# 32 more tokens leave the dense U products, and ScalarE multiplies the gates into the one-hots

## The chip, the cores and the metric

The kernel runs on one core of one Trainium2 chip. The metric is the device time of one execution in microseconds (us); lower is better. Engines are named as in the profile: PE is TensorE (PEld its weight loads), DVE is VectorE, ACT is ScalarE, POOL is GpSimd, SP is the engine that issues most transfers.

## The reference, cut to what matters

512 tokens of width 1024 pass two layers. Each layer is an attention block (three groups of heads) and then a PEER channel mixer. The change touches only the mixer:

```python
q = (xc @ w_q).reshape(c, 8, 2, 128)
sc = einsum('chpd,hpnd->chpn', q, sub_keys)
top_s, top_i = top_k(sc, 16)
cand = top_s[:, :, 0, :, None] + top_s[:, :, 1, None, :]
cand_s, cand_i = top_k(cand.reshape(c, 8, 256), 16)
experts = i1 * 128 + i2                 # 128 of 16384 experts for a token
gates = softmax(cand_s)
ue, ve = u[experts], v[experts]         # rows of 1024 floats
act = gelu(einsum('chkd,cd->chk', ue, xc))
return einsum('chk,chkd->cd', gates * act, ve)
```

Each token uses 128 of the 16384 rows of U and V (8 heads, 16 a head; a "slot" is one of them).

## The kernel before, in words

Tokens lie in four blocks of 128 partitions. Block 0 is computed sparsely: for each of its 128 slots one indirect transfer fetches 128 rows of U (one a token, 512 KB), and VectorE forms the 128 dot products with the tokens in one instruction (`row_dot`, L1508 and L1565). The other 384 tokens (`TN`) are computed densely: all 16384 experts in 128 blocks of 128 (`experts`, L2031). One block is 24 matmuls of 128x128 by 384 columns: eight chunks of the model width, times three products of high and low halves (`stationary`, L2005, L2006, L2009). A block needs its weights from HBM (SP, 512 KB), a cast of them by ScalarE (L979), their remainder by GpSimd (L705), and afterwards a Gelu by ScalarE (`gelu`, L1022), whose result SP stores to `gelu_d` (192 KB).

The order of work in one layer, written out by hand on each engine's queue:

1. The query products and scores; VectorE begins the selection (`unit`, L1423, 32 units: one of a head and a token block). Units 0 to 7 are of block 0, and their row numbers are made at L1494.
2. The PRE stage: 44 pairs of expert blocks on TensorE. VectorE does the other 24 units with four dots of gathered U rows in each (96 slots); GpSimd issues those gathers between its remainders, eight rows in flight (`zone`).
3. The gates: softmax of the chosen scores, `gate_ready` at L1537; TensorE turns the row numbers and the gates of the 384 tokens into columns (L2045), with the last block of the pair (`experts(PRE, 1)`) behind them; ScalarE keeps them in `i_t` and `g_t`.
4. Twelve bodies of 32 tokens (eight groups of four). They write a dense gate matrix: VectorE makes for each token two one-hot rows (`one_hots`, L1549: `oh_2` by L1556, and `oh_1` by L1559, which multiplies the gate in), TensorE multiplies them (`spread`, L2050), ScalarE copies the result to `g_stage` (`keep_gates`, L1061 and L1102). Spreads use two PSUM banks in turn, and the one-hots a ring of four groups. Bodies 0 to 7 (`B_ROUNDS`) also hold four expert blocks each, one after every second group, and four dots of gathered U rows (slots 96 to 127, `gather_b`, `b_row`, four rows in flight). Bodies 8 to 10, here called late, hold two expert blocks each, and ScalarE sets one PSUM bank after each (L1097). Body 11 holds no expert block. In bodies 2 to 9, the staged gates of the window before (two bodies are a window) go to HBM in two transfers of 1 MB a body on ScalarE's queue (L1072).
5. The V stage: 128 blocks of 18 matmuls by 512 columns (L2096), with the gates times the Gelus as stationary operand (`gated`, L1591, reads `h_in` and the gates); block 0's V rows are gathered and added by VectorE (L1615). Then a layer norm.

## Time and profile before

| | |
|---|---|
| Median of 3 runs | 3270.34 us (3270.07 to 3271.58) |
| The profiled execution's own time | 3272.12 us |
| Its span in the profile | 3270.3 us |
| Granted TensorE clock, mean | 0.992 |
| Busy share: PE, PEld, DVE, ACT, POOL | 97%, 88%, 78%, 40%, 60% |
| Moved by transfers | 765.22 MB, mean 234 GB/s |

The busy share of TensorE is modelled from pipelined instructions: each matmul's time overlaps the next one's, so the rate has to be read from start to start. The two layers repeat one pattern; layer 0's mixer fills about 360 to 1625 us of the span, layer 1's about 1990 to 3250 us. PEclk is the granted clock as a share of full speed; the DMA share is the mean busy share of 16 DMA engines.

### The profile page before, as it was taken

What the parts mean: (1) busy time and instruction counts of PE and PEld (TensorE: products, weight loads), DVE (VectorE), ACT (ScalarE), POOL (GpSimd) and SP (SyncE); (2) the same over time, 40 slices, a digit from 0 to 9 for tenths busy, and PEclk for the clock granted to TensorE, in tenths of its full rate; (3) what the DMA queues carried; (4) which work ended last, traced back from release to release, by engine and by line L of the source; (5) the groups of instructions that cost most, each with busy time, mean ns of one, the idle gap of its engine ahead of it and who ended that gap; (6) DMA issues with size and microseconds to landing.
All of it is one profiled execution on the core that took longest, in us unless ns stands there. A gap on an engine that the chain in (4) does not pass through costs nothing. (4 is left out here: it accounts for less than half of the span.)

```text
span 3270.3 us, 64230 instructions
## 1 busy us (share of the span) xinstructions
PE 3173.4 (97%) x18582; PEld 2886.0 (88%) x18582; DVE 2537.1 (78%) x5431; ACT 1306.9 (40%) x2080; POOL 1958.6 (60%) x1556
## 2 busy tenths in 40 slices
PE   8998999999999999999999999999999999999997
PEld 8878889999999888888798787999999998888886
DVE  1475658888888899999925746588888888999998
ACT  2464234444444333333324643344444443333332
POOL 3454348888654466666545543488885535666665
PEclk9999999999999999999999999999999999999999
DMA  4002139999787699999820021499997867999996
GB/s 162 36 2 78 54 107 321 319 320 319 244 297 252 245 338 337 339 335 335 281 103 26 2 78 61 131 320 319 321 319 243 290 241 276 338 338 337 337 333 225
DMA packets 249405, 765.22 MB, mean 234 GB/s; under 512 B 28384, under 2 KB 95712, under 8 KB 241376
## 3 DMA queue, kind: packets, MB, share of 16 engines
q1 hardware_dynamic: 170400, 459.95, 42.6%
q0 software_dynamic: 73728, 268.47, 22.0%
q10 hardware_dynamic: 5184, 35.65, 3.1%
q8 instruction: 47, 0.77, 0.1%
q14 instruction: 46, 0.38, 0.0%
HBM read 677.98 MB, written 85.98 MB: 234 GB/s over the span
## 5 line engine op out<-in xcount | busy, mean ns | idle before, releaser
L705 POOL TENSOR_TENSOR st_lo<-st_raw,st_hi 128x1024 fp32r<-128x1024 f32 x290 | 698.1, 2407 | 463.2 <-ACT st_hi L979 457.4
L979 ACT CAST st_hi<-st_raw 128x1024 fp32r<-128x1024 f32 x544 | 569.9, 1048 | 662.9 <-PE ps L2096 638.0
L2005 PE MATMUL ps<-t_hi,st_hi 128*128 128x384 f32 (+1 forms) x2288 | 794.4, 347 | 0.0
L2006 PE MATMUL ps<-t_lo,st_hi 128*128 128x384 f32 (+1 forms) x2288 | 786.2, 344 | 0.0
L813 POOL TENSOR_TENSOR wt_lo<-w_f,wt_hi 128x384 fp32r<-128x384 f32 x256 | 417.9, 1633 | 319.5 <-ACT wt_hi L1110 319.4
L2009 PE MATMUL ps<-t_hi,st_lo 128*128 128x384 f32 (+1 forms) x2288 | 462.6, 344 | 0.0
L2005 PEld LDWEIGHTS ps<-t_hi,st_hi 128*128 128x128 f32 x2288 | 430.0, 188 | 10.2
L2006 PEld LDWEIGHTS ps<-t_lo,st_hi 128*128 128x128 f32 x2288 | 430.1, 188 | 10.0
L2009 PEld LDWEIGHTS ps<-t_hi,st_lo 128*128 128x128 f32 x2288 | 408.5, 188 | 10.9
L1022 ACT ACTIVATE h_out<-ps 128x384 f32<-128x384 f32 x256 | 125.9, 492 | 695.4 <-PE ps L2009 614.5
L2096 PE MATMUL ps<-st_hi,wt_hi 128*128 128x512 f32 x1536 | 390.6, 390 | 2.7 <-ACT wt_hi L1110 2.7
L2096 PE MATMUL ps<-st_lo,wt_hi 128*128 128x512 f32 x1536 | 390.7, 390 | 0.0
L2096 PE MATMUL ps<-st_hi,wt_lo 128*128 128x512 f32 x1536 | 389.7, 389 | 0.0
L1606 DVE TENSOR_TENSOR st_lo<-st_raw,st_hi 128x1024 fp32r<-128x1024 f32 x252 | 308.8, 1225 | 74.5 <-ACT st_hi L979 74.5
L2096 PEld LDWEIGHTS ps<-st_hi,wt_hi 128*128 128x128 f32 x1536 | 288.5, 188 | 63.5 <-issue 3.7
L2096 PEld LDWEIGHTS ps<-st_lo,wt_hi 128*128 128x128 f32 x1536 | 289.2, 188 | 60.2
L2096 PEld LDWEIGHTS ps<-st_hi,wt_lo 128*128 128x128 f32 x1536 | 288.3, 188 | 59.8
L1615 DVE SCALAR_TENSOR_TENSOR ps<-v_row,w_sp,ps 128x1024 f32<-128x1024 f32 x256 | 326.9, 1277 | 0.5
L1596 DVE TENSOR_TENSOR w_f<-g_ch,h_in 128x256 f32<-128x256 f32 x250 | 303.2, 1213 | 5.2 <-DMA h_in<-gelu_d 3.4
L724 POOL DMA_INDIRECT v_row<-in_peer_v,idx_v x256 | 248.7, 972 | 43.2 <-issue 9.2
L1559 DVE TENSOR_SCALAR oh<-ps,i_t,g_t 128x128 f32<-128x128 f32 x768 | 261.1, 403 | 0.0
L1508 DVE CUSTOM_DVE_ANT_0 u_row<-ps,u_row 128x1024 f32<-128x1024 f32 x192 | 232.3, 1210 | 35.8 <-DMA u_row<-in_peer_ur,idx_u 35.6
(222 smaller groups left out, 4969.1 us busy)
## 6 DMA issues: line engine op xcount, KB each, us to landing
st_raw<-in_peer_u SPq DMA_DIRECT2D x256, 512.0 KB
st_raw<-in_peer_v SPq DMA_DIRECT2D x256, 512.0 KB
gelu_d<-h_out SPq DMA_DIRECT2D x256, 192.0 KB
h_in<-gelu_d SPq DMA_DIRECT2D x256, 192.0 KB
gates_d<-g_stage ACTq DMA_DIRECT2D x32, 1024.0 KB
g_ch<-gates_d SPq DMA_DIRECT2D x56, 512.0 KB, 6.1
w_raw<-in_w_in SPq DMA_DIRECT2D x16, 1168.0 KB, 5.3
st_raw<-in_peer_w_q SPq DMA_DIRECT2D x32, 512.0 KB
```

What stands on the lines that cost most here:

```text
L705: nc.gpsimd.tensor_tensor(st_lo[:, s].rearrange("p c f -> p (c f)"), st_raw[:, r], st_hi[:, s].rearrange("p c f -> p (c f)").bitcast(F32), ...
L724: nc.gpsimd.indirect_dma_start(out=dst, out_offset=None, in_=table, in_offset=bass.IndirectOffsetOnAxis(ap=number, axis=0)).then_inc(lande ...
L813: nc.gpsimd.tensor_tensor(wt_lo[:, s], w_f[:, s], wt_hi[:, s].bitcast(F32), ALU.subtract).then_inc(wt_l, 1)
L979: nc.scalar.copy(st_hi[:, r % 2].rearrange("p c f -> p (c f)"), st_raw[:, r]).then_inc(st_h, 1)
L1559: last = nc.vector.tensor_scalar(oh_1[:, GRP * r + k], iota_ps, i_t[:, 0, ds(t0 + k, 1)], g_t[:, ds(t0 + k, 1)], ALU.is_equal, ALU.mult)
L1596: nc.vector.tensor_tensor(w_f[:, s, 0:T_D].rearrange("p (w o t) -> p w o t", w=2 * WIN_D, o=1), gates, h_in[:, s, 0:T_D].rearrange("p (w o ...
L1606: nc.vector.tensor_tensor(st_lo[:, s].rearrange("p c f -> p (c f)"), st_raw[:, r], st_hi[:, s].rearrange("p c f -> p (c f)").bitcast(F32), ...
L1615: nc.vector.scalar_tensor_tensor(out=acc, in0=v_row[:, r], scalar=w_sp[:, ds(b, 1)], in1=acc, op0=ALU.mult, op1=ALU.add).then_inc(v_acc, 1)
L2005: nc.tensor.matmul(dst, st_hi[:, s, c], t_hi[:, c, rows], start=c == 0, stop=False)
L2006: nc.tensor.matmul(dst, st_hi[:, s, c], t_lo[:, c, rows], start=False, stop=False)
L2009: last = nc.tensor.matmul(dst, st_lo[:, s, c], t_hi[:, c, rows], start=False, stop=c == DC - 1)
L2096: last = nc.tensor.matmul(ps[:, 2 * d + 2 + half], w[:, s, d * P:(d + 1) * P], v[:, half * 512:(half + 1) * 512], start=False, stop=True, ...
```

## The change

The last 32 tokens of block 3 (`XT`) leave the dense U products, which then have 352 columns (`TU`). Their 128 slots are laid out four side by side: partition 32g+t holds slots 32g to 32g+31 of token t, so that 32 more gathers of 128 rows fetch all of them. Dot products go from 128 to 160; the 64 that fall into bodies 0 to 7 are now eight a body. The numbers and the tokens for this layout are moved by eight small transfers from ScalarE's queue before the first body, the results back by four after body 8. Gate times Gelu of those tokens is then put where their gates stood (`g_t`), and their columns of the stored Gelus are ones; the V stage is as before.

The one-hots change hands in part: VectorE makes both rows of a group in one instruction (128x1024, no gate), and ScalarE multiplies the gate into one of them by four activations a group with a pointer as scale (`gate_group`), two groups ahead of its own copy. TensorE's spread waits for ScalarE's (`oh_gated`).

```diff
+XT = 32
+XG = P // XT
+XR = SLOTS // XG
+DOTS = SLOTS + XR
+TU = TN - XT
+BDOTS = 8
+B_ROUNDS = (DOTS - U_ROUNDS * URING) // BDOTS
+X_BODY = (SLOTS - U_ROUNDS * URING) // BDOTS
 KEPT = U_ROUNDS + B_ROUNDS
...
-    oh_2 = gb.tile("oh_2", [P, OH_T, P], F32)
-    oh_1 = gb.tile("oh_1", [P, OH_T, P], F32)
+    oh = gb.tile("oh", [P, OH_G, 2, GRP, P], F32)
...
-                sp.dma_start(gelu_d[2 * i + s], h_out[:, s]).then_inc(s_hst[s], 16)
+                sp.dma_start(gelu_d[2 * i + s], h_out[:, s, 0:TU]).then_inc(s_hst[s], 16)
...
-                sp.dma_start(h_in[:, s], gelu_d[2 * i + s]).then_inc(s_gh[s], 16)
+                sp.dma_start(h_in[:, s, 0:TU], gelu_d[2 * i + s]).then_inc(s_gh[s], 16)
...
-                    pool.wait_ge(u_dot, SLOTS * l + URING * U_ROUNDS + UDOTS * (t - 1) + k + 1)
+                    pool.wait_ge(u_dot, DOTS * l + URING * U_ROUNDS + BDOTS * t + k - UDOTS + 1)
                     pool.sem_inc(waited, 1)
-                gather_rows(b_row[:, k], idx_b[:, half, k:k + 1], a["peer_ur"], s_brow[k])
+                gather_rows(b_row[:, k % UDOTS], idx_b[:, half, k:k + 1], a["peer_ur"], s_brow[k % UDOTS])
 
             def body_blocks(t, half, more=True):
 
-                for k in range(UDOTS):
-                    rest_block((QB + b_body) // 2 + 2 * t + k // 2, (QB + b_body + k) % RAW)
+                for k in range(2):
+                    rest_block((QB + b_body) // 2 + 2 * t, (QB + b_body + k) % RAW)
+                    for n in range(2):
+                        gather_b(t, half, UDOTS + 2 * k + n)
+                for k in range(2):
+                    rest_block((QB + b_body) // 2 + 2 * t + 1, (QB + b_body + 2 + k) % RAW)
                     if k == 0 and more:
                         numbers_b(t + 1, 1 - half)
-                    if k > 0 and more:
-                        gather_b(t + 1, 1 - half, k - 1)
-                if more:
-                    gather_b(t + 1, 1 - half, UDOTS - 1)
+                    for n in range(2 if more else 0):
+                        gather_b(t + 1, 1 - half, 2 * k + n)
...
+            body_blocks(0, 0)
+            body_blocks(1, 1)
+            pool.wait_ge(s_xn, 16 * XG * (l + 1))
+            pool.sem_inc(waited, 1)
+            with pool.Fori(1, B_ROUNDS // 2 - 1) as i:
...
-                nc.scalar.activation(h_out[:, s], ps[:, s, 0:TN], ACT.Gelu).then_inc(gelu_done, 1)
+                nc.scalar.activation(h_out[:, s, 0:TU], ps[:, s, 0:TU], ACT.Gelu).then_inc(gelu_done, 1)
...
+            act.wait_ge(x_numbers, l + 1)
+            for g in range(XG):
+                act.dma_start(idx[g * XT:(g + 1) * XT, SLOTS:DOTS],
+                              idx_x[P - XT:P, g * XR:(g + 1) * XR]).then_inc(s_xn, 16)
+            for g in range(XG):
+                act.dma_start(x_x[g * XT:(g + 1) * XT], x_tok[P - XT:P, TB - 1]).then_inc(s_xx, 16)
...
+            def gate_group(body, g):
+
+                act.wait_ge(oh_ready, TN // GRP * l + GROUPS * body + g + 1)
+                for k in range(GRP):
+                    row = oh[:, g % OH_G, 0, k]
+                    last = nc.scalar.activation(row, row, ACT.Copy, scale=g_t[:, ds(BODY_T * body + GRP * g + k, 1)])
+                last.then_inc(oh_gated, 1)
...
+                        gate_group(body, g + GATE_AHEAD)
                         keep_gates(sw, q, body, g)
...
+            for g in range(GATE_AHEAD):
+                gate_group(0, g)
...
+                        n = w * BODIES + q - B_ROUNDS
+                        if n == 2:
+                            act.wait_ge(x_tr, l + 1)
+                            nc.scalar.copy(g_t[:, TU:TN], ps[:, FREE_BANKS[2], P - XT:P]).then_inc(x_set, 1)
                         stage_body(w, w % 2, q, w < WIN - 1, 1)
-                        n = w * BODIES + q - B_ROUNDS
                         bank = FREE_BANKS[n]
-                        act.wait_ge(acc_open, l + 1)
+                        act.wait_ge(acc_open, 2 * l + 1 + (n == 2))
                         nc.scalar.activation(ps[:, bank], x_tok[:, bank // 2, bank % 2 * T:(bank % 2 + 1) * T], ACT.Copy,
                                              scale=ALPHA).then_inc(acc_set, 1)
+                        if n == 0:
+                            act.wait_ge(dots_kept, KEPT * (l + 1))
+                            nc.scalar.activation(dots[:, SLOTS:DOTS], dots[:, SLOTS:DOTS], ACT.Gelu).then_inc(x_gelu, 1)
+                            act.wait_ge(x_gelu, l + 1)
+                            for g in range(XG):
+                                act.dma_start(h_x[P - XT:P, g * XR:(g + 1) * XR],
+                                              dots[g * XT:(g + 1) * XT, SLOTS:DOTS]).then_inc(s_xh, 16)
...
+                if g + GATE_AHEAD < GROUPS:
+                    gate_group(WIN * BODIES - 1, g + GATE_AHEAD)
...
+            step.done(nc.vector.tensor_copy(e_x[:], e_all[:, UNITS - PH:UNITS].rearrange("p u k -> p (u k)")))
+            step.done(nc.vector.scalar_tensor_tensor(out=idx_f[:], in0=i_all[:, 0, (UNITS - PH) * TOPK:UNITS * TOPK],
+                                                     scalar=float(NK), in1=i_all[:, 1, (UNITS - PH) * TOPK:UNITS * TOPK],
+                                                     op0=ALU.mult, op1=ALU.add))
+            step.wait()
+            nc.vector.tensor_scalar(idx_x[:], idx_f[:], e_base[:, 0:1], None, ALU.add).then_inc(x_numbers, 1)
+            dve.wait_ge(x_numbers, l + 1)
+            step.done(nc.vector.tensor_scalar(e_base[:], e_base[:], float(NEXP), None, ALU.add))
...
-                    nc.vector.tensor_tensor(oh_2[:, GRP * r:GRP * (r + 1)], steps_n,
-                                            i_t[:, 1, ds(t0, GRP)].unsqueeze(2).to_broadcast([P, GRP, P]), ALU.is_equal)
-                    for k in range(GRP):
-                        last = nc.vector.tensor_scalar(oh_1[:, GRP * r + k], iota_ps, i_t[:, 0, ds(t0 + k, 1)],
-                                                       g_t[:, ds(t0 + k, 1)], ALU.is_equal, ALU.mult)
-                    last.then_inc(oh_ready, 1)
-                    if with_dots and g % 2 == 1:
-                        k = g // 2
-                        dve.wait_ge(s_brow[k], 16 * (B_ROUNDS * l + body + 1))
+                    nc.vector.tensor_tensor(oh[:, r], steps_n,
+                                            i_t[:, :, ds(t0, GRP)].unsqueeze(3).to_broadcast([P, 2, GRP, P]),
+                                            ALU.is_equal).then_inc(oh_ready, 1)
+                    if with_dots:
+                        k = g % UDOTS
+                        dve.wait_ge(s_brow[k], 16 * (BDOTS // UDOTS * (B_ROUNDS * l + body) + g // UDOTS + 1))
...
-            assert GROUPS == 2 * UDOTS
-            with dve.Fori(0, B_ROUNDS) as body:
+            assert GROUPS == BDOTS == URING
+            with dve.Fori(0, X_BODY) as body:
                 one_hots(body, True)
-            with dve.Fori(B_ROUNDS, WIN * BODIES) as body:
+            dve.wait_ge(s_xx, 16 * XG * (l + 1))
+            step.done(nc.vector.tensor_copy(x_ps, x_x[:]))
+            step.wait_apart(waited)
+            assert step.n == n_gate
+            at = at + n_gate
+            with dve.Fori(X_BODY, B_ROUNDS) as body:
+                one_hots(body, True)
+            with dve.Fori(B_ROUNDS, B_ROUNDS + 2) as body:
                 one_hots(body, False)
+            dve.wait_ge(s_xh, 16 * XG * (l + 1))
+            nc.vector.tensor_tensor(e_x[P - XT:P], e_x[P - XT:P], h_x[P - XT:P], ALU.mult).then_inc(x_weights, 1)
+            with dve.Fori(B_ROUNDS + 2, WIN * BODIES) as body:
+                one_hots(body, False)
+            nc.vector.memset(h_in[:, :, TU:TN], 1.0)
...
-                stationary(m + QB // 2, s, ps[:, s, 0:TN], slice(P, T))
+                stationary(m + QB // 2, s, ps[:, s, 0:TU], slice(P, P + TU))
...
-                pe.wait_ge(oh_ready, TN // GRP * l + GROUPS * body + g + 1)
+                pe.wait_ge(oh_gated, TN // GRP * l + GROUPS * body + g + 1)
                 for k in range(GRP):
-                    last = nc.tensor.matmul(ps[:, 2 + g % RING, k * P:(k + 1) * P], oh_2[:, GRP * (g % OH_G) + k],
-                                            oh_1[:, GRP * (g % OH_G) + k], start=True, stop=True)
+                    last = nc.tensor.matmul(ps[:, 2 + g % RING, k * P:(k + 1) * P], oh[:, g % OH_G, 1, k],
+                                            oh[:, g % OH_G, 0, k], start=True, stop=True)
...
-            open_sums(FREE_BANKS).then_inc(acc_open, 1)
-            with pe.Fori(B_ROUNDS, WIN * BODIES - 1) as body:
+            open_sums(FREE_BANKS[0:2]).then_inc(acc_open, 1)
+
+            def late_body(body):
+
                 for g in range(GROUPS):
                     spread(body, g)
                     if g % 4 == 3:
                         experts(body + PRE + 1 + B_ROUNDS, g // 4)
+
+            with pe.Fori(B_ROUNDS, B_ROUNDS + 2) as body:
+                late_body(body)
+            pe.wait_ge(x_weights, l + 1)
+            nc.tensor.transpose(ps[:, FREE_BANKS[2], 0:P], e_x[:], ident[:]).then_inc(x_tr, 1)
+            late_body(B_ROUNDS + 2)
+            assert WIN * BODIES == B_ROUNDS + 4
+            pe.wait_ge(x_set, l + 1)
+            open_sums(FREE_BANKS[2:3]).then_inc(acc_open, 1)
```

## Rows read from the trace of the kernel before

**Rows 1.** Windows: us, busy of PE, PEld, DVE, ACT, POOL (count), PEclk, DMA share, GB/s.

```profile
893.60:917.60 24.00, 24.00 (x162) 24.00 (x161) 20.08 (x50) 9.86 (x17) 13.61 (x9) 1.00 0.85 296
1103.00:1106.00 3.00, 3.00 (x9) 2.33 (x8) 0.00 (x0) 0.00 (x0) 2.68 (x4) 0.51 0.99 360
1200.00:1300.00 100.00, 100.00 (x443) 82.81 (x442) 91.73 (x100) 35.16 (x48) 65.97 (x56) 1.00 0.96 339
```

**Rows 2.** TensorE's timeline, 292 and 384 columns (start us, us, engine, line, operation, count).

```profile
29.71 0.30 PE L1713 MATMUL ps<-w_lo,t_hi 128*128 128x292 f32 x1
...
33.19 0.30 PE L1712 MATMUL ps<-w_hi,t_hi 128*128 128x292 f32 x1
...
800.51 0.34 PE L2005 MATMUL ps<-t_hi,st_hi 128*128 128x384 f32 x1
...
803.15 0.34 PE L2006 MATMUL ps<-t_lo,st_hi 128*128 128x384 f32 x1
```

**Rows 3.** VectorE's waits, 480 to 838 us (us in total, times, longest).

```profile
DVE u_row L1508 <- DMA u_row<-in_peer_ur,idx_u: 18.2, 5, 14.1
```

**Rows 4.** VectorE's timeline: the first instruction of two selection units, two units apart.

```profile
706.10 0.42 DVE L1429 TENSOR_TENSOR wk<-scores,ps 128x256 f32<-128x256 f32 x1 [0.27 <-DVE i_all L1481]
...
734.29 0.42 DVE L1429 TENSOR_TENSOR wk<-scores,ps 128x256 f32<-128x256 f32 x1 [0.27 <-DVE i_all L1481]
```

**Rows 5.** TensorE's timeline around the gates (in brackets: idle before, releaser).

```profile
839.75 0.88 PE L2045 MATMUL ps<-ident,i_all 128*128 128x128 f32 x6 [1.07 <-DVE e_all L1537]
...
845.02 1.05 PE L2055 MATMUL ps<-oh,oh 128*128 128x128 f32 x8
846.71 1.13 PE L2055 MATMUL ps<-oh,oh 128*128 128x128 f32 x8 [0.63 <-DVE oh L1559]
```

**Rows 6.** ScalarE's timeline: before the first body, and DMA issues in a body.

```profile
845.81 0.49 ACT L1022 ACTIVATE h_out<-ps 128x384 f32<-128x384 f32 x1 [3.97 <-PE ps L2009]
846.20 1.04 ACT L979 CAST st_hi<-st_raw 128x1024 fp32r<-128x1024 f32 x1
...
894.69 0.95 ACTq L1072 DMA_DIRECT2D gates_d<-g_stage  x2
```

**Rows 7.** VectorE's timeline: making row numbers after the first eight units.

```profile
473.72 1.57 DVE L1494 SCALAR_TENSOR_TENSOR idx_f<-i_all 128x128 f32<-128x128 f32 x1 [0.31 <-DVE i_all L1481]
```

**Rows 8.** Transfers by queue, 893.6 to 1037.6 us: packets, MB, share of 16 engines' time.

```profile
q1 hardware_dynamic: 6916, 17.32, 35.6%
q10 hardware_dynamic: 1728, 12.58, 24.5%
q0 software_dynamic: 2880, 10.49, 20.8%
```

**Rows 9.** A window whose transfers filled its time (columns as rows 1).

```profile
2730.00:2740.00 10.00, 10.00 (x45) 8.24 (x45) 5.03 (x7) 3.23 (x5) 6.52 (x8) 1.00 1.01 386
```

**Rows 10.** Groups by line, 845 to 1090 us (busy us, mean ns of one).

```profile
L1556 DVE TENSOR_TENSOR oh<-ps,i_t 128x512 f32<-128x512 f32 x91 | 62.4, 686 | 32.6 <-PE ps L2055 31.7 <-DVE dots L1570 0.7
...
L1565 DVE CUSTOM_DVE_ANT_0 b_row<-ps,b_row 128x1024 f32<-128x1024 f32 x32 | 38.9, 1216 | 0.0
```

**Rows 11.** ScalarE's timeline in a late body: the gelus that end two halves.

```profile
1063.96 0.49 ACT L1022 ACTIVATE h_out<-ps 128x384 f32<-128x384 f32 x1 [3.64 <-PE ps L2009]
...
1072.24 0.49 ACT L1022 ACTIVATE h_out<-ps 128x384 f32<-128x384 f32 x1 [3.64 <-PE ps L2009]
```

**Rows 12.** ScalarE's groups by form, whole span (busy us, mean ns of one).

```profile
L1010 ACT COPY pq<-ps 128x512 f32<-128x512 f32 x32 | 18.8, 587 | 130.6 <-PE ps L2009 120.3 <-PE ps L2001 10.3
...
L907 ACT ACTIVATE q_a<-ps,sc_s 128x512 fp32r<-128x512 f32 x12 | 8.1, 671 | 0.0
...
L1105 ACT ACTIVATE dots<-dots 128x128 f32<-128x128 f32 x2 | 0.6, 313 | 0.0
```

**Rows 13.** TensorE's timeline: start of the last body, first V product.

```profile
1089.21 1.95 PE L2055 MATMUL ps<-oh,oh 128*128 128x128 f32 x16
...
1102.32 2.32 PE L2096 MATMUL ps<-st_hi,wt_hi 128*128 128x512 f32 x6 [1.37 <-ACT wt_hi L1110]
```

More of the change, by code:

```diff
@@ L94 @@
 OH_G = OH_T // GRP
+GATE_AHEAD = 2
 BODY_T = 32
@@ L286, in build @@
     idx_f = sp_r.tile("idx_f", [P, SLOTS], F32)
-    idx = sp_r.tile("idx", [P, SLOTS], U32)
+    idx = sp_r.tile("idx", [P, DOTS], U32)
+    idx_x = sp_r.tile("idx_x", [P, SLOTS], U32)
+    e_x = sp_r.tile("e_x", [P, SLOTS], F32)
+    h_x = sp_r.tile("h_x", [P, SLOTS], F32)
     idx_u = sp_r.tile("idx_u", [P, 2, URING], U32)
     idx_v = sp_r.tile("idx_v", [P, 2, VRING], U32)
-    idx_b = sp_r.tile("idx_b", [P, 2, UDOTS], U32)
+    idx_b = sp_r.tile("idx_b", [P, 2, BDOTS], U32)
     e_sp = sp_r.tile("e_sp", [P, SLOTS], F32)
     dot_8 = sp_r.tile("dot_8", [P, URING], F32)
-    dots = sp_r.tile("dots", [P, SLOTS], F32)
+    dots = sp_r.tile("dots", [P, DOTS], F32)
     w_sp = sp_r.tile("w_sp", [P, SLOTS], F32)
@@ L309, in build @@
     w_f = vp.tile("w_f", [P, 2, TN], F32)
+    x_x = nc.alloc_sbuf_tensor_at("x_x", [P, D], F32, offset=vp.end)
+    assert vp.end >= tk.end and D <= 4 * TN
     wt_hi = vp.tile("wt_hi", [P, 2, TN], F32R)
@@ L320, in build @@
     gates_d = nc.dram_tensor("gates_d", [P, 2 * WIN_D, NK, WIN_T], F32, kind="Internal").ap()
-    gelu_d = nc.dram_tensor("gelu_d", [EB, P, TN], F32, kind="Internal").ap()
+    gelu_d = nc.dram_tensor("gelu_d", [EB, P, TU], F32, kind="Internal").ap()
     def sem(name):
@@ L371, in build @@
     idx_b_set = sem("idx_b_set")
+    x_numbers, s_xn, s_xx, x_gelu, s_xh, x_weights, x_tr, x_set = (sem(n) for n in (
+        "x_numbers", "s_xn", "s_xx", "x_gelu", "s_xh", "x_weights", "x_tr", "x_set"))
     s_brow = [sem(f"s_brow{r}") for r in range(UDOTS)]
@@ L734, in round_u @@
                     if not first:
-                        pool.wait_ge(u_dot, SLOTS * l + URING * (j - 1) + k + 1)
+                        pool.wait_ge(u_dot, DOTS * l + URING * (j - 1) + k + 1)
                         pool.sem_inc(waited, 1)
@@ L758, in numbers_b @@
             def numbers_b(t, half):
-                nc.gpsimd.tensor_copy(idx_b[:, half], idx[:, ds(URING * U_ROUNDS + UDOTS * t, UDOTS)]).then_inc(
+                nc.gpsimd.tensor_copy(idx_b[:, half], idx[:, ds(URING * U_ROUNDS + BDOTS * t, BDOTS)]).then_inc(
                     idx_b_set, 1)
@@ L787, in _ @@
                 gather_b(0, 0, k, first=True)
-            with pool.Fori(0, B_ROUNDS // 2 - 1) as i:
+            body_blocks(0, 0)
[3 more added lines that the diff above has]
+            with pool.Fori(1, B_ROUNDS // 2 - 1) as i:
                 for half in range(2):
@@ L1104, in _ @@
             act.wait_ge(dots_kept, KEPT * (l + 1))
-            nc.scalar.activation(dots[:], dots[:], ACT.Gelu).then_inc(h_sp, 1)
+            nc.scalar.activation(dots[:, 0:SLOTS], dots[:, 0:SLOTS], ACT.Gelu).then_inc(h_sp, 1)
             def round_gated(b, s):
@@ L1153, in _ @@
         nc.vector.memset(e_base[:], 0.0)
-        n_pre, n_sub, n_unit, n_top, n_idx, n_gate = 4, 1, 23, 6, 2, 5
+        n_pre, n_sub, n_unit, n_top, n_idx, n_gate = 4, 1, 23, 6, 1, 9
         n_ln = 3 * LN_D + 2
@@ L1496, in _ @@
             step.wait()
-            nc.vector.tensor_scalar(idx[:], idx_f[:], e_base[:, 0:1], None, ALU.add).then_inc(idx_ready, 1)
+            nc.vector.tensor_scalar(idx[:, 0:SLOTS], idx_f[:], e_base[:, 0:1], None, ALU.add).then_inc(idx_ready, 1)
             dve.wait_ge(idx_ready, l + 1)
-            step.done(nc.vector.tensor_scalar(e_base[:], e_base[:], float(NEXP), None, ALU.add))
             assert step.n == n_idx
@@ L1544, in _ @@
             step.wait_apart(waited)
-            assert step.n == n_gate
-            at = at + n_gate
-            steps_n = iota_ps.unsqueeze(1).to_broadcast([P, GRP, P])
+            assert step.n == n_gate - 1
+            steps_n = iota_ps.unsqueeze(1).unsqueeze(1).to_broadcast([P, 2, GRP, P])
             def one_hots(body, with_dots):
@@ L1565, in one_hots @@
                         nc.vector.tensor_tensor_reduce(out=b_row[:, k], in0=x_ps, in1=b_row[:, k], scale=1.0, scalar=0.0,
                                                        op0=ALU.mult, op1=ALU.add,
-                                                       accum_out=dot_8[:, k:k + 1]).then_inc(u_dot, 1)
+                                                       accum_out=dot_8[:, g:g + 1]).then_inc(u_dot, 1)
                 if with_dots:
-                    dve.wait_ge(u_dot, SLOTS * l + URING * U_ROUNDS + UDOTS * (body + 1))
@@ L1570, in one_hots @@
-                    nc.vector.tensor_copy(dots[:, ds(URING * U_ROUNDS + UDOTS * body, UDOTS)],
-                                          dot_8[:, 0:UDOTS]).then_inc(dots_kept, 1)
+                    dve.wait_ge(u_dot, DOTS * l + URING * U_ROUNDS + BDOTS * (body + 1))
+                    nc.vector.tensor_copy(dots[:, ds(URING * U_ROUNDS + BDOTS * body, BDOTS)],
+                                          dot_8[:]).then_inc(dots_kept, 1)
                     dve.wait_ge(dots_kept, KEPT * l + U_ROUNDS + body + 1)
@@ L1586, in _ @@
             dve.wait_ge(h_sp, l + 1)
-            nc.vector.tensor_tensor(w_sp[:], dots[:], e_sp[:], ALU.mult).then_inc(w_ready, 1)
+            nc.vector.tensor_tensor(w_sp[:], dots[:, 0:SLOTS], e_sp[:], ALU.mult).then_inc(w_ready, 1)
             dve.wait_ge(w_ready, 2 * l + 2)
```

5 lines of the change are left out of this document (2 added, 3 removed).

## The prediction

> **What bounds the kernel now.** I read the page first: TensorE is busy nearly all the time, so the question is in which stage its work is what the others wait for. The change shortens one kind of TensorE work and adds work to three other units, so each stage was then read by itself.
>
> The windows come next [rows 1]. In a gate body TensorE is busy for all 24.0 us, VectorE for 20.1, and transfers fill 0.85 of their time. In the V stage the transfers run at 0.96, 339 GB/s. The same rows show a stretch at 0.51 of full clock: there TensorE had been idle on and off just before.
>
> Then TensorE's timeline, read from start to start [rows 2]: 384 columns take 2.64/15 = 0.176 us, 292 columns 3.48/26 = 0.134. So the weight loads don't set a floor between the two, and 352 columns take about 0.161. An expert block of 24 matmuls gets shorter by 24 x 0.0147 = 0.35 us. There are 128 blocks a layer; if each saving counted, the kernel would gain 90 us.
>
> In the PRE stage it doesn't count. VectorE waits 18.2 us in 358, 14.1 of them for its first row [rows 3]; a selection unit with its four dots takes 28.19/2 = 14.1 us [rows 4]. GpSimd issues 48 gathers with 40 remainders, so 3.33 blocks go with a unit: 3.33 x 24 x 0.176 = 14.07 us of TensorE. The two are equally long, and at the end TensorE waits 1.07 us for VectorE's gates [rows 5]. The chain of VectorE ends this stage, and the change leaves that chain alone.
>
> **The change, part by part (per layer).**
>
> *PRE stage.* 88 blocks x 0.35 = 31 us less work on TensorE, hidden under VectorE. What remains: the first gather is queued on GpSimd behind remainders that follow TensorE's first U blocks (four of them, 1.4 us), and of the other four waits (4.1 us in all) I take 0.5. Gates 1.9 us earlier; the block behind the transposes is 0.35 shorter: -2.3. Bounds: -0.4 and -5.5 (all of the small waits).
>
> *Before the first body.* Call G the moment the gates are ready (839.7). TensorE ends its block at 845.02 = G+5.3, after the change at G+4.95. VectorE makes the second set of numbers behind G: 1.57 us for the product [rows 7], with the small copies about 2.5. ScalarE waits for that and issues eight transfers at 0.95/2 = 0.475 us [rows 6]: done at G+6.3. The Gelu and the cast are queued behind (0.39 and 0.93 from start to start, the first from [rows 6], the second with the same overlap of 0.10), then the first group of gates. One gate activation: 128x128 without a pointer takes 0.313; a pointer as scale costs 671-587 = 84 ns [rows 12]; less the overlap of 0.10 that [rows 6] show, 0.297 each, 1.19 a group. No row has this instruction; the bounds are 0.21 (no charge for the pointer) and 0.40 (no overlap). The first spread starts 4.0 us after TensorE's block, the second ends at 6.05, against 2.57 before (846.71 + 0.88 - 845.02 [rows 5]): +3.5. TensorE idles 4 us here; as in [rows 1], I expect a stretch at half clock behind it: +1.5 (bounds 0 and 3).
>
> *Bodies 0 to 7.* TensorE: 24.0 - 4 x 0.35 = 22.6 us a body. VectorE a group: one 128x1024 comparison, between 1.22 (a pass of that size, the dot) and 2 x 0.686, and one dot of 1.22 [rows 10]: 8 x 2.6 = 20.7 at most, hidden. ScalarE: 9.9 us [rows 1] + 32 x 0.297 = 19.4, hidden. GpSimd: 13.6 and four more gather issues, hidden unless one took over 2 us. The transfers are another matter. Before, bodies 2 to 7 moved 17.3 MB by SP's queue, 12.6 MB of gates and 10.5 MB gathered, in 80.9% of the time [rows 8]. A full body now moves 4 x 0.524 of weights, 4 x 0.180 of Gelus, 2.10 of gates and 8 x 0.524 gathered: 9.11 MB. By the shares of [rows 8] this is 34.8% + 24.5% + 49.9% = 109% of 24.0 us, 26.2 us. By the V stage's ratio, 339/0.96 = 353 GB/s [rows 1], it is 25.8; at the 386 GB/s of [rows 9] it is 23.6. I take 25.8, since the V stage's mix of reads and gathers is nearest. Bodies 2 to 6 carry the full load, body 7 only half of its gathers, bodies 0 and 1 no gates. So bodies 0 and 1 gain 8 x 0.35 = 2.8 (-2.8), and bodies 2 to 7 take 5 x 25.8 + 22.6 = 151.6 against 144.0: +7.6. Bounds: -8.4 if transfers hide, +12.3 at 26.7.
>
> The Trainium skill speaks against this term (DMA: Bandwidth & Descriptors, section Bandwidth): it measures about 425 GB/s for a core that streams alone. By that a full body needs 21.4 us and hides under 22.6. No stretch of this trace holds such a rate; [rows 9] show 386 at a full share.
>
> *Late bodies 8 to 10.* Here four spread groups go with one block, in 1072.24 - 1063.96 = 8.28 us [rows 11]. With two PSUM banks the third spread waits for ScalarE's copy, which is queued behind Gelu and cast. Now the gates stand in that queue too. From the block's end: Gelu and cast until 1.49; gates 1.19 and copy 0.53, third spread; gates 1.19, copy 0.53 and 0.1 of signalling, fourth spread at 5.0; it takes 0.87, the block 3.97: 9.86. Six halves x 1.58 = +9.4. After body 8 come a small Gelu and four issues of 0.475 with nothing behind them to overlap: +2.4, and +0.4 for the copy of weights ahead of body 10: +12.2. With 0.21 an activation it is +8.2, with 0.40 it is +17.2.
>
> *Body 11.* Before: 13.1 us from its first spread to the first V product [rows 13], its last copy at about 10.8. Now ScalarE has 2.1 us of Gelu, cast and bank, six groups of gates (7.1) and eight copies (4.2): 13.5. +2.7 (bounds +0.8 and +5).
>
> *Elsewhere.* The V stage's instructions don't change, and TensorE fills it [rows 1]: 0. The token block for the four-slot layout is copied by VectorE (about 1.2 us) inside its slack of four groups: 0; with that gone, 1.2.
>
> Sum: -2.3 + 3.5 + 1.5 - 2.8 + 7.6 + 12.2 + 2.7 = +22.4 a layer, +44.8. The profiled execution took 3272.1 us, 1.8 above its span and above the median: 3316.9, and beside the medians **3315**.
>
> **The rivals.**
>
> *A: the transfers hide.* The 386 GB/s of [rows 9] and a share of 0.85 now [rows 1] speak for it, and the page above; against it, five bodies in a row need over 400 GB/s. It decides from 403 GB/s up (9.11 MB in 22.6 us). Then bodies 2 to 7 take 135.6: 16 us less a layer, **3283**.
>
> *B: an activation is cheap*, 0.21 us, as if the pointer were free. Late bodies -4.0, body 11 -1.9, the start -0.7: 13 less in all, **3302**. The pointer's 84 ns [rows 12] speak against it. With A too: 3270.
>
> *C: TensorE sets the pace of the PRE stage.* It and VectorE are equal there to 0.03 us a unit, so VectorE's chain might be what follows. Then 88 x 0.35 - 1.9 = 29 us a layer are won there: 3315 - 58 = **3257**, faster than before. Its place is the unit: it decides from 12.9 us of VectorE a unit down (3.33 x 24 x 0.161). Against it: VectorE has 4.1 us of waits for rows in 24 units after its first, too few to hide 1.2 a unit.
>
> **Chances.** My forecast 0.56, with 3296 to 3342 as its own range (activation and transfer rate at their bounds); A 0.22; B 0.08; A with B 0.05; C 0.05; above 3342 0.04. The range 3280 to 3342 holds the first three. A difference within 0.2% (6.5 us) counts as none. Faster comes from C and a little of A with B: 0.06; the same from A with B: 0.05; slower 0.89.
>
> **What would show it.** PRE: TensorE idles before the transposes by some microseconds more than 1.07, while a unit still takes 14.1 us. Start: TensorE idle 3 to 5 us ahead of the first spread. Bodies 2 to 6: a period of 25 to 26 us, a DMA share near 1.0, waits for `b_row` on VectorE. Late: halves of about 9.9 us, TensorE waiting for ScalarE. The prediction is wrong if the body period is 22.6 (A), if four activations take 0.85 us (B), or if the unit shrinks (C).

## The result, and the profile after

The changed kernel takes 3304.07 us (median of 4 runs, 3300.03 to 3305.78) against 3270.96 for the kernel before on the same chip: a ratio of 1.0099, 95% interval 1.0082 to 1.0117. It is slower by 33 us, inside the range and 11 below the forecast of 3315. The profiled execution has a span of 3303.0 us, 32.7 above that of before, with a mean granted clock of 0.986 (0.992 before).

The page of the changed kernel, its first section and the transfers' totals:

```profile
PE 3117.0 (94%) x18584; PEld 2806.4 (85%) x18584; DVE 2473.3 (75%) x4803; ACT 1523.1 (46%) x2852; POOL 2018.0 (61%) x1620
...
DMA packets 259780, 791.57 MB, mean 240 GB/s; under 512 B 30304, under 2 KB 97632, under 8 KB 251744
```

TensorE has less to do and a smaller share (94% against 97%), ScalarE 46% against 40%, and 26 MB more are moved. No engine has become the bound of the whole, so the loss has to be sought in waits, stage by stage. The starts of the stages, from TensorE's timeline in both traces:

| Layer 0, us | before | after | difference | forecast |
|---|---|---|---|---|
| gates ready, from the span's start | 839.75 | 834.19 | -5.6 | -1.9 |
| gates to the end of the second spread | 7.84 | 13.13 | +5.3 | +4.6 (3.5 + 1.5 - 0.35 for the shorter block) |
| to body 2 | 46.34 | 43.54 | -2.8 | -2.8 |
| bodies 2 to 7 | 144.76 | 147.09 | +2.3 | +7.6 |
| bodies 8 to 10 | 50.52 | 66.68 | +16.2 | +12.2 |
| body 11 to the first V product | 13.11 | 15.93 | +2.8 | +2.7 |
| sum | | | +18.2 | +22.4 |

The end of a spread is taken here as the start of what follows it. In layer 1 the same rows give -8.3 to the gates, +3.7 from there to body 2, +2.1, +14.1 and +2.8: +14.5. The two sums are 32.7, the whole difference of the spans: from the first V product on nothing is lost or gained.

*The gates.* TensorE's timeline where the gates come, the counterpart of [rows 5]:

```profile
834.19 1.54 PE L2109 MATMUL ps<-ident,i_all 128*128 128x128 f32 x6 [8.64 <-DVE e_all L1585]
...
844.45 0.82 PE L2119 MATMUL ps<-oh 128*128 128x128 f32 x5 [3.34 <-ACT oh L1094]
```

The idle before the transposes is 8.64 us and was 1.07: PRE does follow VectorE. Its unit is as long as in [rows 4], (731.52 - 703.22)/2 = 14.15 us:

```profile
703.22 0.42 DVE L1478 TENSOR_TENSOR wk<-scores,ps 128x256 f32<-128x256 f32 x1 [0.27 <-DVE i_all L1530]
...
731.52 0.42 DVE L1478 TENSOR_TENSOR wk<-scores,ps 128x256 f32<-128x256 f32 x1 [0.27 <-DVE i_all L1530]
```

So 31 us less of TensorE's work bring the gates 5.6 us forward. The same six transposes last 1.54 us where they lasted 0.88: behind that idle TensorE runs at half clock (granted clock 0.50 from 834.2 to 838.2).

Of the 5.6 us, 1.0 is a small copy of VectorE just ahead of the gates. In the kernel before it ran beside a remainder of GpSimd, and ended 0.04 us after that; in the changed kernel no remainder runs beside it. VectorE and GpSimd before, then VectorE after:

```profile
833.07 1.22 DVE L1528 COPY c_top<-c_all 128x32 f32<-128x32 f32 x1 [0.32 <-DVE dots L1521]
831.86 2.39 POOL L705 TENSOR_TENSOR st_lo<-st_raw,st_hi 128x1024 fp32r<-128x1024 f32 x1 [1.90 <-ACT st_hi L979]
```

```profile
830.73 0.19 DVE L1576 COPY c_top<-c_all 128x32 f32<-128x32 f32 x1 [0.43 <-DVE dots L1569]
```

*Before the first body.* ScalarE's timeline shows what the first spread waits for (`ACTq` is the engine's queue issuing a transfer):

```profile
836.41 2.51 ACTq L1076 DMA_DIRECT2D idx<-idx_x  x4
838.96 2.67 ACTq L1079 DMA_DIRECT2D x_x<-x_tok  x4
841.73 0.46 ACT L1042 ACTIVATE h_out<-ps 128x352 f32<-128x352 f32 x1 [4.84 <-PE ps L2073]
842.09 1.04 ACT L999 CAST st_hi<-st_raw 128x1024 fp32r<-128x1024 f32 x1
843.02 2.45 ACT L1094 ACTIVATE oh<-oh,g_t 128x128 f32<-128x128 f32 x8
```

The eight issues end 5.2 us after the first began, 0.65 us each (0.475 was forecast). The Gelu, whose input was complete at 841.1, stands behind them, and the gates behind that. Eight activations end 2.45 us after they began: with 0.10 for the last one's overlap, 0.294 each from start to start.

*Bodies 2 to 7.* Windows of body 2 and of a later stretch, as [rows 1], and the waits from 845 to 1035 us:

```profile
893.60:917.60 24.00, 22.00 (x142) 21.72 (x140) 17.58 (x25) 16.90 (x45) 15.76 (x12) 0.93 0.99 370
970.00:990.00 20.00, 20.00 (x136) 19.83 (x135) 15.26 (x21) 15.69 (x41) 15.33 (x12) 1.00 1.02 405
```

```profile
DVE b_row L1617 <- DMA b_row<-in_peer_ur,idx_b: 32.6, 18, 3.2
POOL b_row L738 <- DVE dot L1617: 27.4, 23, 3.7
ACT oh L1094 <- DVE oh L1611: 24.6, 28, 3.2
...
PE ps L2119 <- ACT g_stage L1087: 5.3, 5, 2.0
```

Transfers fill their time (0.85 before), and the wait is handed on: VectorE waits for rows, ScalarE for VectorE's one-hots, TensorE for ScalarE's copy. Of 32.6 us at the first only 5.3 reach TensorE. The transfers from 890.9 to 1037.9 us, by queue, answer to [rows 8]:

```profile
DMA packets 15197, 53.28 MB, mean 362 GB/s; under 512 B 1692, under 2 KB 4802, under 8 KB 13656
...
q0 software_dynamic: 6477, 23.57, 41.7%
q1 hardware_dynamic: 6987, 17.08, 32.6%
q10 hardware_dynamic: 1728, 12.58, 21.3%
```

The megabytes are the forecast's (five times 9.11 and 7.0 are 52.6). The rate is 362 GB/s over the stretch at a share of 0.96, and 405 in the window above. Bodies 2 to 6 take 24.65 us each on average, where 25.8 was forecast.

*Late bodies.* ScalarE's Gelus at the ends of two halves, the counterpart of [rows 11], and between them one group:

```profile
1094.67 0.46 ACT L1042 ACTIVATE h_out<-ps 128x352 f32<-128x352 f32 x1 [2.78 <-PE ps L2073]
...
1097.61 1.28 ACT L1094 ACTIVATE oh<-oh,g_t 128x128 f32<-128x128 f32 x4
1098.79 0.57 ACT L1087 COPY g_stage<-ps 128x512 f32<-128x512 f32 x1
...
1104.60 0.46 ACT L1042 ACTIVATE h_out<-ps 128x352 f32<-128x352 f32 x1 [1.94 <-PE ps L2073]
```

9.93 us a half (four spread groups and one block), 9.86 forecast, 8.28 before. After body 8 a half lasts 15.96. The same half before took 8.89, since ScalarE sets a PSUM bank in it, from this Gelu to the first of [rows 11]:

```profile
1055.07 0.49 ACT L1022 ACTIVATE h_out<-ps 128x384 f32<-128x384 f32 x1 [3.63 <-PE ps L2009]
```

So this half is 7.1 us longer, where 1.6 + 2.4 = 4.0 was forecast. ScalarE there, and TensorE's next spread:

```profile
1059.30 0.22 ACT L1141 ACTIVATE dots<-dots 128x32 f32<-128x32 f32 x1
1059.55 2.48 ACTq L1144 DMA_DIRECT2D h_x<-dots  x4
1062.07 0.20 ACT L1055 ACTIVATE warm<-eps 128x1 f32<-128x1 f32 x1 [2.55 <-issue]
1062.10 1.04 ACTq L1106 DMA_DIRECT2D gates_d<-g_stage  x2
1063.24 1.28 ACT L1094 ACTIVATE oh<-oh,g_t 128x128 f32<-128x128 f32 x4 [0.97 <-issue]
```

```profile
1065.05 3.79 PE L2119 MATMUL ps<-oh 128*128 128x128 f32 x16 [5.82 <-ACT g_stage L1087]
```

From the small Gelu to the first gates ScalarE spends 3.94 us. Of these, 1.04 go to the two issues of the staged gates, which before stood beside the cast (at 1055.22 and 1055.59). By the copy that TensorE waits for it has been idle for 5.82 us, and its sixteen spreads last 3.79 us where 1.95 is usual: half clock, and a granted clock of 0.60 between 1062 and 1070.

### The profile page after: what moved, and what is told of

It reads as the page before. It is cut to its first block and busy times, and to the rows that moved or that the text cites. A ratio compares the mean times of both kernels' runs of the same rounds, so it can differ in the third digit from the quotient of the medians.

```text
span 3303.0 us, 64288 instructions
## 1 busy us (share of the span) xinstructions
PE 3117.0 (94%) x18584; PEld 2806.4 (85%) x18584; DVE 2473.3 (75%) x4803; ACT 1523.1 (46%) x2852; POOL 2018.0 (61%) x1620
## 5 line engine op out<-in xcount | busy, mean ns | idle before, releaser
L2069 PE MATMUL ps<-t_hi,st_hi 128*128 128x352 f32 (+1 forms) x2288 | 764.8, 337 | 10.0 <-ACT st_hi L999 9.5
L2070 PE MATMUL ps<-t_lo,st_hi 128*128 128x352 f32 (+1 forms) x2288 | 753.4, 331 | 0.0
L2073 PE MATMUL ps<-t_hi,st_lo 128*128 128x352 f32 (+1 forms) x2288 | 435.5, 332 | 17.1 <-POOL st_lo L719 16.3
L2073 PEld LDWEIGHTS ps<-t_hi,st_lo 128*128 128x128 f32 x2288 | 380.0, 188 | 37.0 <-POOL st_lo L719 26.0
L1042 ACT ACTIVATE h_out<-ps 128x352 f32<-128x352 f32 x256 | 118.8, 464 | 467.4 <-DMA gelu_d<-h_out 318.1
L1611 DVE TENSOR_TENSOR oh<-ps,i_t 128x1024 f32<-128x1024 f32 x192 | 232.7, 1221 | 93.5 <-PE ps L2119 84.4
L1094 ACT ACTIVATE oh<-oh,g_t 128x128 f32<-128x128 f32 x768 | 245.9, 394 | 51.8 <-DVE oh L1611 48.9
```

The source lines that it names most:

```text
L1094: last = nc.scalar.activation(row, row, ACT.Copy, scale=g_t[:, ds(BODY_T * body + GRP * g + k, 1)])
L2069: nc.tensor.matmul(dst, st_hi[:, s, c], t_hi[:, c, rows], start=c == 0, stop=False)
L2070: nc.tensor.matmul(dst, st_hi[:, s, c], t_lo[:, c, rows], start=False, stop=False)
L2073: last = nc.tensor.matmul(dst, st_lo[:, s, c], t_hi[:, c, rows], start=False, stop=c == DC - 1)
```

## The experiments

Ten kernels were run. In the diffs `...` stands for lines left out. Ratios are to the kernel before, each time on the same chip; its median was between 3270.6 and 3271.4.

**One group further ahead.** If the gates wait for nothing but their place in the queue, more lead should help.

```diff
-GATE_AHEAD = 2
+GATE_AHEAD = 3
```

> The changed kernel with ScalarE gating three groups ahead of its copy instead of two. My theory: in a late half the third spread waits for Gelu, cast, four gate activations and a copy, in that order, while ScalarE stood idle for about 1.9 us before the Gelu; with one group more gated in that idle time a half loses 1.2 us, 7 us a layer: 3290 us (3284 to 3294). Rival: what binds late is the sum of ScalarE's work, whatever its order: 3304, within 3 us. A second rival: waits for one-hots one group further ahead hurt bodies 0 to 7, where gathered rows come late: 3304 or above.

Measured: 3350.93 us, ratio 1.0245 (1.0228 to 1.0262), 47 us slower than with two. A miss. The late half is still 9.86 us: the third spread waits for a copy, and one group of gates stands ahead of it in the queue whatever the lead. In the bodies with gathers the lead does harm: bodies 2 to 7 take 166.9 us in layer 0, not 147.1. The waits from 890 to 1067 us, which are those bodies:

```profile
DVE b_row L1617 <- DMA b_row<-in_peer_ur,idx_b: 32.9, 11, 4.8
ACT oh L1094 <- DVE oh L1611: 29.6, 14, 3.0
...
PE ps L2119 <- ACT g_stage L1087: 21.0, 12, 3.6
```

With a lead of two, the same bodies show 27.3 us of VectorE's wait for rows and 5.3 of TensorE's for the copy; here it is 32.9 and 21.0. The granted clock falls with the idles, to 0.94 over these bodies from 0.99. By the order of the queue, ScalarE now waits for one-hots a group nearer to what VectorE is making, and the copy that TensorE needs stands behind.

**Gates by ScalarE, nothing else.** The kernel before, with the gates in ScalarE's activations, and still 384 columns.

```diff
+            def gate_group(body, g):
+                act.wait_ge(oh_ready, TN // GRP * l + GROUPS * body + g + 1)
+                for k in range(GRP):
+                    row = oh[:, g % OH_G, 0, k]
+                    last = nc.scalar.activation(row, row, ACT.Copy, scale=g_t[:, ds(BODY_T * body + GRP * g + k, 1)])
+                last.then_inc(oh_gated, 1)
...
+                        gate_group(body, g + GATE_AHEAD)
                         keep_gates(sw, q, body, g)
...
```

> The kernel before with one half of the change alone: VectorE makes both one-hots of a group in one instruction, ScalarE multiplies the gates in; all 384 tokens stay dense, nothing more is gathered. My theory: start +2.3, six late halves +1.9 each, body 11 +2.8: +16.6 us a layer, 3304 us (3296 to 3310), by chance as long as the whole change. Rival: the gates on ScalarE are hidden and the added gathers make the loss: 3271, within 5 us.

Measured: 3311.95 us, ratio 1.0131 (1.0114 to 1.0148). The late half is 10.19 us (the Gelus stand at 1052.95 and 1063.14), two others 11.7 and 12.4 with TensorE at half clock, and bodies 0 to 7 keep their 6.00 us for two groups and a block: there the gates cost nothing. This half of the change costs 41 us, more than the whole, and 2 us above the expected range: the start took 3.6 us a layer where 2.3 was expected, bodies 8 to 10 13.7 where it was 11.4.

**352 columns, nothing else.** The kernel before with 352 columns, and nothing computed for the 32 tokens.

```diff
+TU = TN - 32
...
-                stationary(m + QB // 2, s, ps[:, s, 0:TN], slice(P, T))
+                stationary(m + QB // 2, s, ps[:, s, 0:TU], slice(P, P + TU))
```

> The kernel before with the other half reduced to its gain: the U products have 352 columns, and nothing is put in the place of the last 32 tokens (their Gelus count as one, so their outputs are not the reference's). My theory: the PRE stage ends with VectorE, about 5.6 us earlier than before, less 1.5 for a slow clock behind the idle time; 38 blocks behind the gates give 0.35 each: -17 us a layer, 3236 us (3230 to 3246). Rival: TensorE sets the pace everywhere and all 128 blocks count: 3181. Rival below: nothing is won since other engines bind: 3271.

Measured: 3230.31 us (3225.11 to 3241.19), ratio 0.9888 (0.9871 to 0.9906): -41 us, the most that could be gained, where 256 blocks x 0.35 us would be 90. TensorE is idle for 8.65 us before the gates, as in the changed kernel. The two halves cancel (+41 and -41). If they add, which no run shows by itself, the 33 us that remain are what the 32 tokens themselves cost: their issues, their gathers and what follows from them.

**PRE at 384 columns.** The changed kernel, but its 88 PRE blocks a layer keep all columns.

```diff
-                    experts(i, s)
+                    pe.wait_ge(gelu_done, EB * l + 2 * i + s + 1)
+                    stationary(i + QB // 2, s, ps[:, s, 0:TN], slice(P, T))
```

> The changed kernel with the 88 PRE blocks at 384 columns (the last 32 columns of each are computed and not used). Theory: the PRE stage follows VectorE's chain, so that 31 us of TensorE's work a layer come back almost for nothing: the gates are later by some of the 5.6 us that they had gained, and TensorE, which then idles less before them, loses less to the slow clock behind them: +4 a layer, 3312 us (3306 to 3317). Rival, TensorE paces the stage too: all 88 x 0.35 = 31 us a layer count, 3366.

Measured: 3313.88 us, ratio 1.0129 (1.0114 to 1.0145): +9.8, not +62. TensorE's timeline at the gates:

```profile
838.76 0.87 PE L2110 MATMUL ps<-ident,i_all 128*128 128x128 f32 x6 [1.46 <-DVE e_all L1585]
...
848.54 1.83 PE L2120 MATMUL ps<-oh 128*128 128x128 f32 x7 [4.77 <-ACT oh L1094]
```

With 31 us more of work the gates come 4.6 us later, the transposes run at full clock again, and VectorE's chain waits 2.9 us for ScalarE's exponentials, as before and unlike the changed kernel (0.7). Rival C is out.

**Late gates back to VectorE.** From group 2 of body 8 on VectorE multiplies the gates in, as before.

```diff
...
+                    else:
+                        nc.vector.tensor_tensor(oh[:, r, 1], iota_ps.unsqueeze(1).to_broadcast([P, GRP, P]),
+                                                i_t[:, 1, ds(t0, GRP)].unsqueeze(2).to_broadcast([P, GRP, P]), ALU.is_equal)
+                        for k in range(GRP):
+                            last = nc.vector.tensor_scalar(oh[:, r, 0, k], iota_ps, i_t[:, 0, ds(t0 + k, 1)],
+                                                           g_t[:, ds(t0 + k, 1)], ALU.is_equal, ALU.mult)
+                        last.then_inc(oh_ready, 1)
...
```

> The changed kernel, but from the third group of body 8 on VectorE multiplies the gates in itself, as before the change; bodies 0 to 7 as changed. My theory: ScalarE's gates cost about 16 us in bodies 8 to 10 and 3 us in body 11 of each layer, of which some 3 us (the four issues after body 8) stay: -16 us a layer, 3272 us (3266 to 3280). Rival: the loss of the change sits in the gathers of bodies 0 to 7: then this gives less than 8 us in all, 3296 or above.

Measured: 3278.21 us, ratio 1.0023 (1.0013 to 1.0032). Late halves are 7.5 to 8.6 us again, and of the 33 us 26 are back. The half after body 8 is still 15.0, with TensorE idle for 4.65:

```profile
1060.46 3.78 PE L2133 MATMUL ps<-oh 128*128 128x128 f32 x16 [4.65 <-ACT g_stage L1087]
```

**And the four late transfers to SP.** In the kernel of the run above, ScalarE's four issues after body 8 go to SP's queue as well.

```diff
-                            for g in range(XG):
-                                act.dma_start(h_x[P - XT:P, g * XR:(g + 1) * XR],
-                                              dots[g * XT:(g + 1) * XT, SLOTS:DOTS]).then_inc(s_xh, 16)
...
+                if b == EB - 5:
+                    sp.wait_ge(x_gelu, l + 1)
+                    for g in range(XG):
+                        sp.dma_start(h_x[P - XT:P, g * XR:(g + 1) * XR],
+                                     dots[g * XT:(g + 1) * XT, SLOTS:DOTS]).then_inc(s_xh, 16)
```

> The changed kernel with the late gates multiplied in by VectorE (as in the run before, 3278) and the four transfers after body 8 issued by SP in place of ScalarE. Theory: the 5 us of idle and the slow clock behind them come from ScalarE standing in its issues; without them the half after body 8 falls from 15.0 us to about 9: 6 a layer, 3266 us (3260 to 3270). Rival, the issues are not what TensorE waits for there: 3278.

Measured: 3268.61 us, ratio 0.9993 (0.9984 to 1.0002). Between two Gelus lie 8.56 us, with no stall:

```profile
1052.48 0.46 ACT L1047 ACTIVATE h_out<-ps 128x352 f32<-128x352 f32 x1 [3.22 <-PE ps L2085]
...
1061.04 0.46 ACT L1047 ACTIVATE h_out<-ps 128x352 f32<-128x352 f32 x1 [3.22 <-PE ps L2085]
```

So four issues cost 9.6 us of the time: 2.5 us each layer as issues, the rest as idle and slow clock behind them.

**Copy first.** The gates stay with ScalarE, but its copy of a group goes ahead of the gates of a later one in bodies 8 to 11.

```diff
-                        gate_group(body, g + GATE_AHEAD)
+                        if pairs == 2:
+                            gate_group(body, g + GATE_AHEAD)
                         keep_gates(sw, q, body, g)
+                        if pairs == 1:
+                            gate_group(body, g + GATE_AHEAD + 1)
...
```

> The changed kernel with ScalarE's copy of a spread group put ahead of the gates of a later one in bodies 8 to 11 (the gates there run three groups ahead). Theory: in a late half the third and fourth spread wait for a copy that stands behind gates in ScalarE's queue; with the copy first, a half falls from 9.86 us to about 8.7, near ScalarE's own sum of 4 x (1.18 + 0.53) + 1.5 = 8.4: six halves, 7 us a layer, 3290 us (3284 to 3297). Rival, the gates themselves and not their order set the half: 3304.

Measured: 3290.37 us, ratio 1.0059 (1.0042 to 1.0076). A late half, on TensorE's timeline from one first spread to the next, is 1057.49 - 1048.72 = 8.77 us:

```profile
1048.72 1.95 PE L2124 MATMUL ps<-oh 128*128 128x128 f32 x16
1050.86 1.16 PE L2124 MATMUL ps<-oh 128*128 128x128 f32 x8 [0.19 <-ACT g_stage L1087]
1052.50 1.16 PE L2124 MATMUL ps<-oh 128*128 128x128 f32 x8 [0.48 <-ACT g_stage L1087]
...
1057.49 0.72 PE L2124 MATMUL ps<-oh 128*128 128x128 f32 x5
```

It was the order in the queue that cost 1.1 us a half. The 0.9 us that remain above the 7.83 of a half with VectorE's gates go with ScalarE's activations themselves.

**Half of the gathers.** In bodies 0 to 7 the second four dots of a body read the rows of the first four.

```diff
             def gather_b(t, half, k, first=False):
+                if k >= UDOTS:
+                    return
...
```

> The changed kernel without half of the gathers in bodies 0 to 7: the second four dots of each body read the four rows of the first four again, so that 2.1 of 9.1 MB a body are left out and VectorE's work is the same. Theory: bodies 2 to 7 are held up by transfers alone; without the load they run at TensorE's pace, 6 x 22.35 = 134 us in place of 147: 3304 - 26 = 3278 us (3275 to 3284). Rival, ScalarE's gates or VectorE's longer queue hold TensorE up there: bodies 2 to 7 stay near 147, 3304.

Measured: 3290.58 us (3284.55 to 3296.61), ratio 1.0054 (1.0038 to 1.0069): -13.5, half of what was expected, and outside the range. The profile is of the slowest execution. Windows of bodies 2 to 7:

```profile
891.93:1031.09 139.16, 139.16 (x964) 138.88 (x963) 112.96 (x148) 114.35 (x295) 77.44 (x49) 1.00 0.83 289
```

TensorE has no gap left, the transfers have room (0.83), the clock is full, and yet these bodies take 139.2 us, not 134. The block itself is longer. TensorE's timeline in the changed kernel, the second and the sixteenth matmul of a block, and the same two in this one:

```profile
870.46 0.32 PE L2070 MATMUL ps<-t_lo,st_hi 128*128 128x352 f32 x1
...
872.68 0.32 PE L2070 MATMUL ps<-t_lo,st_hi 128*128 128x352 f32 x1
```

```profile
870.75 0.33 PE L2075 MATMUL ps<-t_lo,st_hi 128*128 128x352 f32 x1
...
873.09 0.33 PE L2075 MATMUL ps<-t_lo,st_hi 128*128 128x352 f32 x1
```

2.22/14 = 0.159 us from start to start in the one, 2.34/14 = 0.167 in the other, at the same granted clock: a cycle (two groups and a block, a quarter of a body) takes 5.59 or 5.78 us. In layer 0 of this run every block behind the first two has the longer one until body 7 ends: 24 cycles x 0.19 = 4.6 of the 5.1 us that bodies 2 to 7 lie above 134. In layer 0 the changed kernel begins with 5.59, goes to 5.78 after its first stall, at 905 us, and back and forth later.

**320 columns, nothing else.** As with 352 columns alone, but 64 tokens left out. The edit is shown against that kernel.

```diff
-TU = TN - 32
+TU = TN - 64
```

> The kernel before with 320 columns in the dense U products and nothing computed in place of the 64 tokens. Theory: a matmul of 352 columns has two paces (0.159 and 0.167 us from start to start), of which the bodies keep the one that they fell into; 320 columns take 0.0133 us less than the quicker, 40 blocks a layer outside PRE are shorter by 0.32 us more than with 352, and the 88 blocks of PRE count nothing: 3230 - 26 = 3204 us (3198 to 3212). Rival, the second pace belongs to a limit beside the columns (weight loads), so that 320 columns come out little better than 352: 3215 to 3225.

Measured: 3201.60 us, ratio 0.9785 (0.9769 to 0.9802), 29 us below 352 columns alone and inside the expected range. One pace throughout, (869.63 - 867.58)/14 = 0.146 us:

```profile
867.58 0.31 PE L2008 MATMUL ps<-t_lo,st_hi 128*128 128x320 f32 x1
...
869.63 0.31 PE L2008 MATMUL ps<-t_lo,st_hi 128*128 128x320 f32 x1
```

**The start as well.** The late gates with VectorE, the late transfers with SP, the eight early issues spread over the blocks of bodies 0 and 1, and the first two groups of gates ahead of PRE's last Gelu.

```diff
+                    if w == 0:
+                        move_x(2 * pairs * q + b)
...
                 gate_group(0, g)
+            gelu_last()
```

> As the kernel whose late gates are on VectorE and whose four late transfers are SP's, and also: the eight transfers ahead of the first body are issued one after each expert block of bodies 0 and 1, and the first two groups of gates stand ahead of the last Gelu of PRE. Theory: TensorE's 3.3 us of idle before the first spread and the slow clock behind go: about 4.4 a layer less than that kernel, 3257 us (3250 to 3263), and so below the kernel before (3271). Rival, the issues cost TensorE the same wherever they stand in ScalarE's queue: no gain, 3266.

Measured: 3262.69 us (3258.16 to 3267.92), ratio 0.9976 (0.9965 to 0.9987): below the kernel before by 0.24%. It is 6 us below the run without it, where 9 was expected, and the two runs' ranges overlap. From the gates to the end of the second spread it takes 11.0 us (13.4 without), and TensorE's first spread no longer waits, though its second does:

```profile
845.03 1.05 PE L2144 MATMUL ps<-oh 128*128 128x128 f32 x8
847.75 1.13 PE L2144 MATMUL ps<-oh 128*128 128x128 f32 x8 [1.66 <-ACT oh L1103]
```

## Why the prediction was right, point by point

*PRE.* Right in kind: VectorE's chain sets it, shown by the 352 columns alone (8.65 us of idle) and by PRE at 384 columns (+9.8 us in all). The size was off: -1.9 was forecast, -5.6 came. In VectorE's rows the wait for U rows fell from 18.2 to 15.8 us, that for the exponentials from 2.9 to 0.7 (ScalarE's queue was free earlier, which I had not looked at), and a copy of 128x32 from 1.22 to 0.19 us. The first two are TensorE's 31 us after all: others waited for what it finished, and with PRE at 384 columns they come back (17.3 and 2.9). The third depends on what GpSimd does beside it, as shown above. In the kernels' traces each such copy that was long (0.9 to 1.75 us) ended 0.04 to 0.05 us after a remainder of GpSimd that had begun before it. No run moved the remainder alone.

*Start.* +4.6 forecast, +5.3 measured, in other parts. The issues took 0.65 us each, not 0.475. VectorE's product took 0.29, not 1.57: the 1.57 of [rows 7] is again a case of a remainder beside it (GpSimd's ended at 475.15, the product at 475.29), so that row was no price for the product by itself. The slow clock came twice: behind the idle of 8.64 us as well, which my sum did not hold because it held no such idle.

*Pitch*, the time from one matmul's start to the next. 0.161 taken, 0.159 measured, and sometimes 0.167, which no row of before shows. At the quicker one a body takes 22.35 us (352 columns alone), not 22.6.

*Bodies 0 and 1:* -2.8 and -2.8.

*Bodies 2 to 7.* That the gathers hold these bodies up is shown: with half of them gone they fall from 147.1 to 139.2 us and TensorE waits no more, while ScalarE's gates alone leave them at 144.8, as before. The gathers are not all of it. With 352 columns alone they take 134.8; of the 12.3 us above that, half of the gathers gives back 7.9, and the other 4.4 are, in that run's trace, the slower pitch, which my sum did not hold. The term was mis-sized, +7.6 against +2.3 (against +2.1 in layer 1), at the step "By the V stage's ratio, 339/0.96 = 353 GB/s". The same ratio in this stretch is 362/0.96 = 377 GB/s, and 9.11 MB at that rate are 24.2 us a body where I had 25.8; 24.65 was measured. Rival A, the transfers hide, is out, and was further off: 135.6 was its price for these bodies, 151.6 mine, 147.1 measured. The Trainium skill (DMA: Bandwidth & Descriptors, section Bandwidth) gives about 425 GB/s for a core that streams alone; single slices of this stretch, 3.7 us long, reach 425, the stretch does not.

*Late bodies.* The half was right, 9.93 against 9.86, and so was its cause: putting the copy first takes 1.1 us off a half, VectorE's gates take all of it off. The activation, which no row of before had, lies at 0.294 (0.297 forecast), so rival B is out. The Trainium skill (ScalarE: Activation LUTs, section What ACT_TABLE_LOAD costs) gives 186 ns + 0.833 ns an element, 93 for a pointer and 93 of overlap between neighbours; for 128 elements this is 293 ns, and the trace agrees. What failed is the step "four issues of 0.475 with nothing behind them to overlap: +2.4". ScalarE was late by 3.94 us, and I had put no slow clock behind it: the half grew by 5.5 us beyond the 1.6 of a common half (4.5 in layer 1). The first half of body 10, with 1.95 us of idle and a slow clock, grew by 0.9 beyond it (0.4 forecast).

*Body 11:* +2.7 and +2.8.

Forecast less measured, the errors were +3.7, -0.7, +5.3, -4.0 and -0.1 us in layer 0 and partly cancelled. In layer 1, gates to body 2 taken together, they were +6.4, -1.9, +5.5, -1.9 and -0.1. The sign of each term was right and the late bodies were the largest loss; but bodies 2 to 7, which I had put second, came out as the smallest term, and the gain of PRE as the second. The closeness of 3304 to 3315 owes something to that cancelling.

## What to carry to other kernels

Work taken from a busy engine is worth what its stage waits for: of a layer's 128 blocks made shorter, the 88 beside VectorE's chain gave 5 to 10 us of 31 (PRE at 384 columns, 352 columns alone), the 40 others 15, all that was forecast for them (14), where nothing else held them up (352 columns alone). Work given to an idle engine costs the engine that waits for something behind it in its queue: gates and twelve small issues on a ScalarE that is busy 46% of the time cost more than the 32 tokens saved. So put what others wait for first, issue small transfers from a queue in which nothing is awaited, and give the gates to whichever engine is free in that stage.
